# Sixteen modulation chunks of a two-layer transformer kernel, moved into an attention tile

## The reference

```python
for l in range(DEPTH):
    sh_a, sc_a, gt_a, sh_f, sc_f, gt_f = silu(c) @ w_mod[l] + b_mod[l]       # the same for c_ctx
    hl = rmsnorm(xl) * g_attn[l] * (1 + sc_a) + sh_a                          # and hc from xc
    out_lat, out_ctx = token_mixers(hl, hc, ...)      # w_in, four kinds of attention, w_out
    xl = xl + gt_a * out_lat
    hl = rmsnorm(xl) * g_ffn[l] * (1 + sc_f) + sh_f
    xl = xl + gt_f * expert_choice_ffn(hl, ...)       # 16 experts, each takes its best tokens
    ...                                               # context likewise, in layer one only
return rmsnorm(xl) * g_final
```

## Time and profile before

| what | value |
|---|---|
| median of 3 runs | 2147.86 us |
| the profiled execution's own time | 2151.53 us |
| its span, first to last instruction | 2149.7 us |
| mean granted TensorE clock | 0.975 |
| PE busy | 1969.2 us (92%) |
| DVE, ACT, POOL busy | 664.1, 529.6, 156.6 us |
| read from HBM | 498.69 MB |

### The profile page before, as it was taken

How to read it: one execution, slowest core, us unless ns; L and a number is a source line. 1 busy time by engine, 2 the same in 40 slices (tenths; PEclk the granted TensorE clock), 3 DMA queues, 4 the chain that set the end, 5 groups by cost and what they waited for, 6 DMA issues and landing times. The chain is left out here.

```text
span 2149.7 us, 27244 instructions
## 1 busy us (share of the span) xinstructions
PE 1969.2 (92%) x10872; PEld 931.5 (43%) x10872; DVE 664.1 (31%) x1746; ACT 529.6 (25%) x1222; POOL 156.6 (7%) x155
## 2 busy tenths in 40 slices
PE   5999989999979999999999899889997998888875
PEld 2436465556642332323323556455554333333322
DVE  3322345666540100101001632366665011110203
ACT  3211154665531000100100421165554110000001
POOL 1101010000010010020100101100001000000000
PEclk9999979999989999999999999999998999999998
DMA  9742020000089999999999402020017899999995
GB/s 353 291 159 81 0 79 1 1 2 1 36 332 414 423 364 418 378 390 421 364 414 421 150 20 79 17 82 1 21 40 286 352 427 426 426 427 427 427 427 217
DMA packets 90935, 515.66 MB, mean 240 GB/s; under 512 B 10594, under 2 KB 15628, under 8 KB 36540
## 3 DMA queue, kind: packets, MB, share of 16 engines
q1 hardware_dynamic: 84496, 493.29, 56.8%
q0 software_dynamic: 4416, 15.21, 2.4%
q10 hardware_dynamic: 1900, 5.43, 0.6%
HBM read 498.69 MB, written 15.20 MB: 239 GB/s over the span
## 5 line engine op out<-in xcount | busy, mean ns | idle before, releaser
L739 PE MATMUL psS<-arena 128*64 128x512 f32 (+9 forms) x4552 | 1158.5, 556 | 71.1 <-DMA arena<-in_w_up 22.0
L739 PEld LDWEIGHTS psS<-arena 128*64 128x64 f32 (+4 forms) x4552 | 456.1, 159 | 666.9 <-issue 585.9
L1961 DVE TENSOR_REDUCE mx<-psS 128x1 f32<-128x768 f32 (+2 forms) x200 | 165.5, 827 | 153.0 <-PE psS L739 151.3
L1307 ACT ACTIVATE arena<-psT 128x768 f32<-128x768 f32 (+7 forms) x261 | 150.1, 577 | 245.7 <-PE psT L742 232.0
L742 PE MATMUL psT<-ident,arena 128*128 128x128 f32 (+1 forms) x1036 | 172.7, 290 | 36.1 <-ACT arena L1307 9.1
L1307 ACT ACTIVATE arena<-psS 128x128 f32<-128x128 f32 (+5 forms) x158 | 61.8, 421 | 571.6 <-PE psS L739 525.7
L2145 DVE TENSOR_TENSOR arena<-arena,psS 128x512 f32<-128x512 f32 x32 | 20.6, 684 | 549.2 <-PE psS L739 549.2
L742 PEld LDWEIGHTS psT<-ident,arena 128*128 128x128 f32 (+1 forms) x1036 | 120.1, 145 | 135.5 <-issue 97.8
L739 PE MATMUL psT<-arena 128*32 128x512 f32 x1536 | 174.5, 595 | 0.0
L1307 ACT ACTIVATE arena<-psS,nb 128x768 f32<-128x768 f32 (+2 forms) x200 | 157.9, 792 | 1.4
L739 PE MATMUL psM<-arena 128*128 128x512 f32 x288 | 140.9, 611 | 0.0
(11 more groups left out here) (226 smaller groups left out, 1266.5 us busy)
## 6 DMA issues: line engine op xcount, KB each, us to landing
arena<-in_w_gate SPq DMA_DIRECT2D x117, 1024.0 KB, 21.3
arena<-in_w_up SPq DMA_DIRECT2D x116, 1024.0 KB, 22.5
arena<-in_w_down SPq DMA_DIRECT2D x116, 1024.0 KB, 25.9
arena<-in_w_mod SPq DMA_DIRECT2D x48, 1024.0 KB, 7.2
arena<-in_w_in SPq DMA_DIRECT2D x6, 2048.0 KB, 7.8
arena<-in_w_out SPq DMA_DIRECT2D x8, 512.0 KB, 7.8
arena<-in_w_out SPq DMA_DIRECT2D x2, 2048.0 KB, 15.4
normed_rows<-arena ACTq DMA_DIRECT2D x8, 512.0 KB, 7.3
```

The lines of the kernel that those rows point to most:

```text
L739: return nc.tensor.matmul(o, lhsT, rhs, start=start, stop=stop)
L1307: return nc.scalar.activation(o, i, f, **kw)
L1961: link(V.reduce_max(mx[:, par:par + 1], view(S, 0, P, 0, (512, 2), (1, n)), axis=AX.XY))
```

## The change

The last two groups of modulation chunks leave the expert ring. They are loaded into four slots in the space of `w_in` and, later, `w_out` (`late_slot`): chunks 0 and 1 of the sixteen when the fourth section is projected, 2 and 3 when the fifth is, and each further one when the chunk four before it has been multiplied. PE multiplies them at steps 0 to 11 of the first context tile of layer one (`LATE_AT`), into banks 7 and 5. ACT copies the two rows at steps 6 and 12, PE transposes them at steps 16 and 24 and DVE copies the columns there. The router's bias moves from steps 3 and 5 to 7 and 8, the gates from 7, 9, 11, 13 to 9, 11, 13, 15. `w_out` is loaded in four parts, each when its slot's last chunk has been multiplied. All steps of groups 4 and 5 in layer one's routing, in `combine` and in layer two's projections go. Layer one's ring holds expert chunks alone, without the wait for the third gather. In layer two the last two of the ring's 17 slots are first loaded when the second gather has landed. The diff, without its context and without lines that only drop `FIRST` or an unused part:

```diff
@@ -58,8 +57,8 @@
-GATE_AT = ((7, 9, 11, 13), (9, 11))
-BIAS_AT = ((3, 5), (7,))
+GATE_AT = ((9, 11, 13, 15), (9, 11))
+BIAS_AT = ((7, 8), (7,))
...
@@ -182,9 +181,11 @@
-MOD_LATE, MOD_LAST = KD, KD
-assert (MOD_FRONT * KD + MOD_LATE + MOD_LAST) == 3 * L * KD
-LAST_MOD_AT = {"turn": 13, "columns": 14}
+LATE_AT = {0: (0, 1), 1: (2, 3), 2: (4,), 3: (5,), 4: (6,), 5: (7,), 7: (8, 9), 8: (10, 11), 9: (12,), 10: (13,), 11: (14, 15)}
+LATE_ROW_AT = {6: 0, 12: 1}
+LATE_TURN_AT = {TURNS: 0, TURNS + 8: 1}
+LATE_BANK, LATE_TURN_BANK = (7, 5), 5
+LATE_SLOTS = 4
...
@@ -428,19 +429,18 @@
-        MOD_FILLS = [MOD_FRONT if i < KD else 0 for i in range(max(NSLOT))]
+        MOD_FILLS = [L * 3 if i < KD else 0 for i in range(max(NSLOT))]
-        FIRST, LAST = (MOD_LATE, 0), (MOD_LAST, 0)
-            j += FIRST[l]
-            earlier = MOD_FILLS[i] + sum(i < NSLOT[k] and (FIRST[k] + NLOAD + LAST[k] - 1 - i) // NSLOT[k] + 1 for k in range(l))
+            earlier = MOD_FILLS[i] + sum(i < NSLOT[k] and (NLOAD - 1 - i) // NSLOT[k] + 1 for k in range(l))
-        def late_bank(g):
-            return 7 if g == MOD_FRONT else 3
+        def late_slot(c):
+            return WOUT + (4096, 6144, 0, 2048)[c % LATE_SLOTS]
...
@@ -574,6 +574,13 @@
+                def late_chunk(c):
+                    _, r, k = MOD_CHUNKS[MOD_FRONT * KD + c]
+                    if c >= LATE_SLOTS:
+                        sp.wait_ge(s_mused, MOD_FRONT * KD + c - LATE_SLOTS + 1)
+                    load(ar[:, late_slot(c):late_slot(c) + SLOT], A["w_mod"][L - 1, k * P:(k + 1) * P, r * 2048:(r + 1) * 2048], s_w[c % 8])
...
@@ -594,16 +601,28 @@
+                if l == 0:
+                    sp.wait_ge(z["proj"], NSTEP - TT)
+                    for c in range(2):
+                        late_chunk(c)
-                for k, w in ((0, A["w_out"][l, 0:256, :]), (6, A["w_out"][l, 768:1024, :])):
-                    for b in range(2):
-                        load(view(ar, 64 * b, 64, WOUT + k * D, (D, 2), (1, D)),
-                             w[128 * b:128 * b + 128, :].rearrange("(a p) n -> p a n", p=64), z["wo"])
-                load(ar[:, WOUT + 2 * D:WOUT + 6 * D].rearrange("p (k n) -> p k n", k=4),
-                     A["w_out"][l, 256:768, :].rearrange("(k p) n -> p k n", p=P), z["wo"])
-                for j in range(FIRST[l] + NLOAD + LAST[l]):
+                if l == 0:
+                    for c in range(2, 2 * KD):
+                        late_chunk(c)
+                for n, k in enumerate((4, 6, 0, 2)):
+                    if l == 0:
+                        sp.wait_ge(s_mused, (MOD_FRONT + 2) * KD - LATE_SLOTS + n + 1)
+                    w = A["w_out"][l, k * P:(k + 2) * P, :]
+                    if k in (0, 6):
+                        for b in range(2):
+                            load(view(ar, 64 * b, 64, WOUT + k * D, (D, 2), (1, D)),
+                                 w[128 * b:128 * b + 128, :].rearrange("(a p) n -> p a n", p=64), z["wo"])
+                    else:
+                        load(ar[:, WOUT + k * D:WOUT + (k + 2) * D].rearrange("p (k n) -> p k n", k=2),
+                             w.rearrange("(k p) n -> p k n", p=P), z["wo"])
+                for j in range(NLOAD):
...
@@ -614,21 +633,14 @@
+                        sp.wait_ge(s_g[1], 16 * L)
-                    if l == 0 and j == FIRST[l] + AHEAD_OF_GATHER:
-                        sp.wait_ge(s_g[2], 16)
-                    if 0 <= last < FIRST[l]:
-                        sp.wait_ge(s_mused, MOD_FRONT * KD + last + 1)
-                    elif last >= 0:
-                        st, e = divmod(last - FIRST[l], QUAD)
+                    if last >= 0:
+                        st, e = divmod(last, QUAD)
-                    if j < FIRST[l] or j >= FIRST[l] + NLOAD:
-                        _, r, k = MOD_CHUNKS[MOD_FRONT * KD + (j if j < FIRST[l] else j - NLOAD)]
-                        load(ring(l, j), A["w_mod"][L - 1, k * P:(k + 1) * P, r * 2048:(r + 1) * 2048], s_w[j % NSLOT[l]])
-                        continue
-                    n = j - FIRST[l]
+                    n = j
...
@@ -779,17 +791,16 @@
-            def late_mod(n):
-                j, g, k = n - MOD_FRONT * KD, n // KD, n % KD
-                b = late_bank(g)
-                if j >= FIRST[0]:
-                    j += NLOAD
-                pe.wait_ge(*slot_filled(0, j - FIRST[0]))
+            def late_mod(c):
+                n, g, k = MOD_FRONT * KD + c, c // KD, c % KD
+                b = LATE_BANK[g]
+                pe.wait_ge(s_w[n % 8], 16 * (n // 8 + 1))
-                    mm(bank(b), ident[:, :], modrow[:, g * 512:(g + 1) * 512], True, False)
-                for c in range(4):
-                    last = mm(bank(b, 32 * c, 32), scm[:, k * 32:(k + 1) * 32], ring(0, j, c * 512, 512), False, k == KD - 1)
+                    mm(bank(b), ident[:, :], modrow[:, (MOD_FRONT + g) * 512:(MOD_FRONT + g + 1) * 512], True, False)
+                for j in range(4):
+                    a = late_slot(c) + j * 512
+                    last = mm(bank(b, 32 * j, 32), scm[:, k * 32:(k + 1) * 32], ar[:, a:a + 512], False, k == KD - 1)
...
@@ -856,7 +867,7 @@
-                        pe.wait_ge(z["wo"], 80 * (l + 1))
+                        pe.wait_ge(z["wo"], 96 * (l + 1))
...
@@ -1006,6 +1013,7 @@
+                        pe.wait_ge(s_mrow, MOD_FRONT + 1)
...
@@ -1108,6 +1116,14 @@
+                    for c in LATE_AT.get(s, ()) if l == 0 else ():
+                        if c == KD:
+                            pe.wait_ge(z["me"], turns_through(PLANS[l], ("Q", 1, "B1")))
+                        late_mod(c)
+                    if l == 0 and s in LATE_TURN_AT:
+                        g = LATE_TURN_AT[s]
+                        pe.wait_ge(z["me"], turns_through(PLANS[l], ("Q", 2, "B1") if g else ("Q", 1, "C1")))
+                        mod_transpose(MOD_FRONT + g, LATE_TURN_BANK)
...
@@ -1120,6 +1136,10 @@
+                        if l == 0 and x == ("Q", 1, "D"):
+                            pe.wait_ge(s_mrow, MOD_FRONT + 2)
+                        if l == 0 and x in (("T", 0, None), ("Q", 2, "D")):
+                            pe.wait_ge(s_mcol, MOD_FRONT + (1 if x[0] == "T" else 2))
...
@@ -1162,21 +1182,12 @@
-                late = range(MOD_FRONT * KD, (MOD_FRONT + 1) * KD) if l == 0 else ()
-                for n in late[:6]:
-                    late_mod(n)
-                    if n and l == 0:
-                        late_mod(late[6])
-                for n in late[7:]:
-                    late_mod(n)
-                for g in (MOD_FRONT,) if l == 0 else ():
-                    mod_transpose(g, late_bank(g))
...
@@ -1218,10 +1228,6 @@
-                        if l == 0 and n == 2 * TC:
-                            pe.wait_ge(z["y"], hidden_tile(l, q, NX - 1))
-                            for m in last_late[:4]:
-                                late_mod(m)
...
@@ -1233,8 +1239,6 @@
-                    for m in last_late[4:] if l == 0 else ():
-                        late_mod(m)
...
@@ -1331,8 +1335,8 @@
-                act.wait_ge(s_mused, KD * (g + 1))
-                a_(modrow[:, g * 512:(g + 1) * 512], bank(late_bank(g))).then_inc(s_mrow, 1)
+                act.wait_ge(s_mused, KD * (MOD_FRONT + g + 1))
+                a_(modrow[:, (MOD_FRONT + g) * 512:(MOD_FRONT + g + 1) * 512], bank(LATE_BANK[g])).then_inc(s_mrow, 1)
...
@@ -1533,6 +1535,8 @@
+                    if l == 0 and s in LATE_ROW_AT:
+                        modulation_row(LATE_ROW_AT[s])
...
@@ -2003,6 +2003,8 @@
+                    if l == 0 and s in LATE_TURN_AT:
+                        mod_columns(MOD_FRONT + LATE_TURN_AT[s], LATE_TURN_BANK)
```

More of the change, by code:

```diff
@@ L35 @@
 NQ = NE // QUAD
-AHEAD_OF_GATHER = 6
 COMBINED = ((NQ - 1,), tuple(range(NQ)))
@@ L979, in _ @@
                         scores(0)
-                    if l and tau == 3:
-                        pe.wait_ge(s_mrow, 3 * L)
-                    if l and tau == LAST_MOD_AT["turn"]:
-                        mod_transpose(MOD_FRONT + 1, 5)
                     for i in k_jobs(tau - 1):
@@ L1211, in turn_hidden @@
                         free[6 + b] = (z["he"], 2 * hidden_tile(l, q, g) - 1 + b)
-                last_late = range((MOD_FRONT + 1) * KD, len(MOD_CHUNKS))
                 def combine(q):
@@ L1267, in group @@
                                 a = src + (2 * kq + k) * W + col + e * n
-                                r = ring(l, FIRST[l] + (q * NSTAGE + st) * QUAD + e, k * D + h * 512, 512)
+                                r = ring(l, (q * NSTAGE + st) * QUAD + e, k * D + h * 512, 512)
                                 p0 = n * (e - experts[0])
@@ L1379, in _ @@
                         modulated_low(t)
-                    if l and tau == 2:
-                        modulation_row(MOD_FRONT + 1)
                     if l == 0 and tau == LAM_AT[1]:
@@ L1575, in _ @@
                 second_list_reversed()
-                if l == 0:
```

(6 more changed lines are left out.)

## The result

| | before | after |
|---|---|---|
| median, us | 2147.95 (7 runs) | 2155.77 (7 runs) |
| lowest to highest | 2144.3 to 2151.38 | 2153.74 to 2160.12 |
| ratio of after to before, 95% interval | | 1.0034 [1.002, 1.0048] |
| the profiled execution: its time, span, mean clock | 2151.53, 2149.7, 0.975 | 2160.12, 2158.3, 0.978 |

The change costs 7.8 us. The range (2140 to 2160) holds it, and the forecast's own (2145 to 2156) does so at its edge; the likeliest case, 2151.5, was 4.3 us short, and at 0.34% the result lies just beyond the 0.3% that I called no change (the interval reaches to both sides of that line).

The account below looks back on a forecast made before the run. Layer one's experts were taken as PE-bound, layer two's as load-bound; +11.3 - 2.1 - 0.6 - 2.5 - 2.5 = +3.6 us gave 2155.1 for the profiled execution, 2151.5 for the median, range 2140 to 2160.

Parts of the forecast that it names:

- What bounds the stages: Expert stages: layer one's bound by PE, layer two's by loading; removing chunks from layer one's gives at most 4.4 us.
- E: Tile 0, the first context tile of layer one's attention: multiplies added, less waits and clock gained, +11.3 us.
- The clock term: In tile 0, 2.4 GHz returns near 280 as wide multiplies replace narrow ones: 6.4 us gained, bounds 0 and 8.0.
- The waits: In tile 0, 3.5 us of PE's waits for ACT disappear; new waits for chunks and the row copy add 1.8.
- the sign that E is wrong: Tile 0 should end 10 to 12 us later; growth under 7 us or over 16 would refute E.
- R1: Rival, slower: tile 0's clock stays at 1.2 GHz as long, PE thinly busy; E 17.7, sum +10.0, 2157.9; chance 0.20.
- R2: Rival, faster: tile 0's added work nearly free, full relief elsewhere; E +7.2, some -8 in all, 2140; chance 0.18.
- A: End of layer one's experts: latent combine 1.1 us sooner, layer two's first transposes 2.4 sooner; -2.1 us.
- B: Layer two: transposes leave a PE-bound projection, 0.5 us, and ACT's row copy goes, 0.1; -0.6 us.
- C: Layer one's routing: three fewer chunks loaded ahead of the gathers, so gathers land and experts start sooner; -2.5 us.
- D: Layer two's last two slots: loads held back behind the gathers, which land sooner; -2.5 us, bounds 0 and -3.6.
- R3: Rival, slower: gathers in both layers get no faster, so C and D are nothing; +8.6 us, 2156.5; chance 0.10.

Follow-up runs that it names:

- D undone: The changed kernel without layer two's wait for the second gather: 2158.89 us, ratio 1.0047 to the kernel before.
- three loads beside the gathers: The changed kernel with the last three loads of layer one's first ring round held back to run beside the gathers: 2160.85 us, ratio 1.0063.
- A alone: The kernel before with the last group's eight chunks, in layer one's combine, multiplied over 32 of their 512 columns: 2146.0 us, ratio 0.9986.
- D alone: The kernel before with only layer two's wait for the second gather added: 2145.76 us, ratio 0.9989.

## Why the prediction was right or wrong

- **What bounds the stages: right.** Layer one's experts last 542.12 us at the same PE busy time, as the earlier trace rows, and its ring without sixteen chunks gives nothing back there. One reading was wrong: "DMA is empty there" does not hold for the first part of tile 0, where the earlier trace rows have a share of 1.00 from 273 to 277 and 0.45 from 280 to 293.
- **E, +11.3: the size about right, by luck; the working was wrong in three terms.** The changed kernel's own execution has 13.6; the two other executions with the same tile 0 (D undone, three loads beside the gathers) have 10.8 and 13.8. The multiplies cost what I had them at: the eleven groups at 2.4 GHz are 16.0 by their rows. The clock term failed: the return near 280 came, but with the falls at 288, 305 and 312, which I had not seen, it is worth 1.5 us in tile 0 and not 6.4. The waits failed: I took 1.7 off (3.5 of ACT less 1.8 of new ones), and PE's idle time grew by 0.5. So tile 0 grew by 17.8, past the bound of 16 that I gave as the sign that E is wrong. That R1 has 17.7 is chance: it has PE thinly busy and the clock low as long as before, but the earlier trace rows have PE busy for 13.00 of 13 us at 0.50, and PE waited for one chunk only. Then 4.2 came back in the second tile, where two low stretches of before (from 317.6 and from 358.5, 6.8 us each) are missing. No term of mine stands for that, and with A alone, where nothing in these tiles was changed, 2.7 came back too. And the loads: I priced the landing of single chunks, 1.0 us with bounds of 0 and 9, and never set 14 chunks at 427 GB/s against the length of the tile. That limit is about as high as that of the multiplies, and with the work nearly free, as R2 wanted it, it held E near 10 in the one trace that shows it (9.8).
- **A, -2.1: wrong, under 1 us.** The combine came the 1.1 sooner; the step that failed is that layer two's first transposes then start 2.4 sooner (0.7 in the profiled execution, 0.9 at most). Behind 3.7 us of idle PE the combine starts at 1.2 GHz, its sums come late to DVE, and the next root, from DVE and POOL, sets the pace.
- **B, -0.6: right at the place, the rest open.** 0.47 went at the transposes as worked out, and 0.4 to 0.5 in all eight executions without them. The profiled one loses 0.6 in layer two's first attention steps, where PE's waits for ACT rose from 6.0 to 7.5 us. But that stretch moves by -1.9 to +1.4 in executions of kernels in which nothing was changed there, so whether B stays is not shown.
- **C, -2.5: -1.7.** The gathers gained 2.9, more than the 2.5 that I took; two short waits of PE took 0.6, not the low clock that I named, and late chunks 0.6. What I had wrong is why it works: I credited three fewer loads, and a kernel with three fewer loads and the same ring lost 4 to 5 us. The full ring is the condition, as far as these two fillings (three chunks and eleven) can show it.
- **D, -2.5: right, -2.7** by the trace, 3.1 and 2.0 by the two timings. "The held-back loads fit into the gap" stands: PE gained 4.0, and the 1.3 that it gave back at a load near 1770 it gave back without the wait too.
- **The rule on queues.** The Trainium skill (DMA: Bandwidth & Descriptors, Queues, rings and completion order) has every DMA engine take turns between the queue rows, a packet at a time, from which I estimated 1.2 us for a gather beside loads. Here the traces do not agree with that estimate: a gather beside loads lands 3.0 us later in layer two (7.7 and 4.7) and 1.8 or 3.9 later in layer one (7.1 in the kernel before and 9.2 with three loads held back, against 5.3). The estimate took the shares of the two queues to be equal; whether that or something else is wrong no run shows.
- **The rivals.** R3 is out. R1 had the tile's length and not its reasons; R2 failed with E and A. By the parts: E came out 2.3 higher than summed, A, B, C together 3.4 less of a gain, D 0.2 more, and the start and the end of the execution -0.5: 3.6 + 2.3 + 3.4 - 0.2 - 0.5 = 8.6.

A version that beats both, by little, is the kernel before with D alone: 2145.76, 0.9989 [0.998, 0.9999].

## What to carry to other kernels

Work that moves into a stage takes its loads along: set their bytes over the bandwidth against the length of that stage, before pricing the landing of one. When an edit takes work away and nothing gets faster, look for a second limit of the same height; a two by two (work with and without, loads with and without) finds it in four kernels. Gathers beside bulk loads landed 1.8 to 3.9 us later here, but in layer one holding the loads back paid where the ring was full ahead of the gathers and cost 4 to 5 us where it held three chunks.

## What the runs showed that I had not expected

The clock in one and the same piece of program is not the same from run to run. Four more executions have the tile 0 of the kernel before, with the same multiplies in the same order. Three show the 1.2 GHz level for 20.5, 20.5 and 17.1 us from 272 to 278 on, and the one with 32 columns in the combine, some 900 us later, for 10.2 only; its stretches:

```profile
277.00:284.00 7.00, 7.00 (x40) 6.36 (x40) 1.52 (x7) 2.44 (x10) 0.00 (x0) 0.50 1.04 282
284.00:297.00 13.00, 11.21 (x100) 7.75 (x96) 5.75 (x23) 7.83 (x25) 0.79 (x2) 0.98 0.19 76
```

That execution passes tile 0 and the next 6.4 us faster than the profiled one of before, with nothing changed there. The changed kernel's tile 0 does the same: two executions have 17.1 us at the low level and grow by 17.8 and 17.9, the third (D undone) has 6.8 and grows by 13.6. The falls at 288 and 312 are missing in the third. So a few microseconds of a single trace at such a place are no evidence; the medians and the repeats are. The Trainium skill (TensorE: Matmul & The Clock Gate, Part 1: The HAM clock gate) says that the number of slow multiplies at the start of a kernel varies between runs of it. The traces agree, for a stretch in the middle of a kernel, with 10.2 to 20.5 us here.

And work that is taken away can cost clock: the latent combine ran at 2.4 GHz in all four executions in which four modulation chunks, multiplied in full, stood right ahead of it, and for some 3 us or more at 1.2 in all nine in which PE idled there for 2.1 to 3.7 us.
